# Hybrid decoder trunk: last stage's sums in PSUM on TensorE, and expert routing in two batches of four tiles

## The reference, cut to what matters

```python
x = x + mem_cross_attention(h, memn, w_mq, w_mkv, w_mo)
h = rmsnorm(x, norm_ffn)
# hier_moe: top-1 of 4 groups, then top-2 of the 8 experts in it
grp_prob = softmax(h @ w_rg + b_rg); p_grp, g_sel = top_k(grp_prob, 1)
sel = (h @ w_re + b_re) of the selected group
w_top, i_top = top_k(softmax(sel), 2); w_top /= sum(w_top)
gates = p_grp * w_top;  idx = g_sel * 8 + i_top
out = sum over the two chosen experts e of gates_e * (silu(h @ wg_e) * (h @ wu_e)) @ w_dn_e
x = x + out
return rmsnorm(x) * norm_final
```

## Time and profile before

| | |
|---|---|
| median of 3 runs | 1349.31 us |
| the profiled execution | 1345.35 us |
| its span | 1343.5 us |
| TensorE busy | 1187.0 us, 88% of the span |
| VectorE busy | 505.0 us, 38% |
| ScalarE busy | 395.5 us, 29% |
| GpSimd busy | 130.8 us, 10% |
| mean granted TensorE clock | 0.949 |

### The profile page before, as it was taken

One profiled execution on the slowest core, in us unless ns is written; L12 is line 12 of the kernel. 1 busy time (PEld: TensorE's weight loads), 2 busy tenths in 40 slices (PEclk: granted clock), 3 DMA queues, 4 the chain that ended last, 5 costly groups with the idle time before them and its releaser, 6 DMA issues.

```text
span 1343.5 us, 17627 instructions
## 1 busy us (share of the span) xinstructions
PE 1187.0 (88%) x7200; PEld 659.5 (49%) x7200; DVE 505.0 (38%) x1224; ACT 395.5 (29%) x753; POOL 130.8 (10%) x126
## 2 busy tenths in 40 slices
PE   5899999999999999997899998677759999999940
PEld 4444744447545898874554444345533333333310
DVE  5322314111798256754512221256632221222118
ACT  3102631113684231136641000474201111111115
POOL 1000011110000000011000000211011111111024
PEclk9799999999999999998999999799769999999975
DMA  5311112221125433303040003410149999999536
GB/s 178 110 32 33 32 53 75 75 75 53 32 71 242 114 80 123 119 2 126 1 157 1 0 0 131 188 48 32 48 173 417 412 417 416 423 418 412 218 151 257
DMA packets 67450, 199.55 MB, mean 149 GB/s; under 512 B 25780, under 2 KB 42404, under 8 KB 56612
## 3 DMA queue, kind: packets, MB, share of 16 engines
q1 hardware_dynamic: 59328, 181.39, 35.3%
q0 software_dynamic: 7456, 16.92, 3.3%
q10 hardware_dynamic: 580, 0.05, 0.0%
HBM read 172.63 MB, written 35.14 MB: 155 GB/s over the span
## 4 chain that ended last, share of the span: by engine, by line
PE 82%; DVE 9%; ACT 3%; issue 3%; DMA 2%; ACTq 0%; POOL 0%; DVEq 0%; POOLq 0%
PE bank L2285 28%; PE bank L1414 12%; PE bank L1475 7%; PE bank L1440 6%; PE bank L750 2%; PE bank L736 2%; PE bank L1490 2%; PE bank L1530 2%; PE bank L1400 2%; PE bank L2393 2%; PE bank L811 1%; PE bank L783 1%; PE bank L2274 1%; PE bank L841 1%; DVE arena L1661 1%
## 5 line engine op out<-in xcount | busy, mean ns | idle before, releaser
L2285 PE MATMUL bank<-arena 128*128 128x512 f32 (+3 forms) x1088 | 379.4, 509 | 1.6 <-DVE arena L2090 1.6
L2285 PEld LDWEIGHTS bank<-arena 128*128 128x128 f32 x1088 | 206.5, 191 | 169.3 <-issue 154.4
L1414 PE MATMUL bank<-arena 128*32 128x512 f32 x1536 | 171.0, 597 | 2.0 <-DVE arena L1193 2.0
L1414 PEld LDWEIGHTS bank<-arena 128*32 128x32 f32 x1536 | 50.7, 111 | 117.1 <-issue 117.1
L1866 ACT ACTIVATE arena<-bank 128x512 f32<-128x512 f32 (+1 forms) x64 | 32.9, 514 | 226.3 <-PE bank L2285 226.0
L1475 PE MATMUL bank<-arena 128*128 128x512 f32 x220 | 95.6, 592 | 0.0
L1440 PE MATMUL bank<-arena 128*32 128x512 f32 x768 | 87.4, 595 | 0.7 <-ACT arena L1102 0.7
L1202 DVE TENSOR_TENSOR arena<-arena,bank 128x256 f32<-128x256 f32 x25 | 10.5, 421 | 168.8 <-ACT arena L1098 155.7
L1475 PEld LDWEIGHTS bank<-arena 128*128 128x128 f32 x220 | 41.3, 190 | 49.7 <-issue 49.7
L1854 ACT ACTIVATE arena<-arena 128x1024 f32<-128x1024 f32 x26 | 27.4, 1054 | 127.2 <-DVE arena L1262 106.2
L1262 DVE TENSOR_TENSOR arena<-arena,bank 128x512 f32<-128x512 f32 x32 | 22.0, 688 | 112.5 <-PE bank L1475 87.8
(11 more groups left out here) (372 smaller groups left out, 1634.9 us busy)
## 6 DMA issues: line engine op xcount, KB each, us to landing
arena<-in_w_e_gu SPq DMA_DIRECT2D x27, 2048.0 KB, 15.8
arena<-in_w_e_dn SPq DMA_DIRECT2D x33, 1024.0 KB
arena<-in_w_in SPq DMA_DIRECT2D x11, 1024.0 KB, 5.4
arena<-y_d SPq DMA_DIRECT2D x8, 1024.0 KB, 5.0
arena<-hz_d SPq DMA_DIRECT2D x4, 1792.0 KB, 8.1
arena<-in_w_e_gu SPq DMA_DIRECT2D x6, 1024.0 KB
arena<-in_w_e_gu SPq DMA_DIRECT2D x12, 512.0 KB
pk_d<-arena SPq DMA_DIRECT2D x8, 640.0 KB, 2.9
```

Source lines behind the costliest of these rows:

```text
L1414: ins = mm(bank[part, :], hgT[:, k, part], w_gu(es[i] % NB, k), start=(k == 0), stop=(k == KT - 1))
L2285: ins = mm(psum[PROJ_BANKS[u % 3]][0:rows, 0:n], lhs(k), rhs(k), start=(k == 0), stop=(k == KT - 1))
```

## The change

Routing keeps its arithmetic and is cut in two batches of BT = 4 tiles. `route(m)` ends with the experts' maxima and indices. `choose(b)` makes the expert numbers and one-hot rows of four tiles at once; `ranks(b)` gets the ranks of four tiles by one product with the triangle and products of ones with the counts of each earlier tile, in banks 5 and 6; `place_tokens(b)` does the placing for four tiles in operations four times as wide; `table(b)` sums 8 products in bank 1, which holds the whole table at the end. `choose(0)` stands at the end of VectorE's step 8, `ranks(0)` at the end of TensorE's step 9, `place_tokens(0)` in step 11 behind the last normed rows and before `route(7)`. After the loop TensorE does the products for the earlier tiles of batch 1, `table(0)`, `ranks(1)`, the totals and `table(1)`. `probs_transposes(it)` moves ahead of `out_product(it-2, 1)`.

In the last stage VectorE makes `w_diag[m]`, diagonal matrices of the first gate. TensorE puts x2 into a bank by a product with the identity and adds the first expert's rows by a product with `w_diag[m]`. VectorE combines the second expert's rows with the bank, in two halves. ScalarE's `weigh` and GpSimd's add are gone.

```diff
             def route(m):
                 dve.wait_ge(s["t_rl"], m + 1)
-                link(v.tensor_tensor(lg[:, m], psum[7][:, 0:NR], br, ALU.add))
+                v.tensor_tensor(lg[:, m], psum[7][:, 0:NR], br, ALU.add).then_inc(s["t_slt"], 1)
+                dve.wait_ge(s["t_slt"], m + 1)
...
+            def choose(b):
+                ms = slice(BT * b, BT * b + BT)
+                link(v.tensor_copy(sixb, six[:, ms, 0:TK]))
+                link(v.scalar_tensor_tensor(eid_all[:, ms], bc(gself[:, ms], 2, [P, BT, TK]), float(EPG), sixb,
                                             ALU.mult, ALU.add))
+                link(v.tensor_tensor(oh, bc(io_f[:, 0:NE], 1, [P, BT * TK, NE]),
+                                     bc(flat(eid_all[:, ms]), 2, [P, BT * TK, NE]), ALU.is_equal))
+                v.tensor_tensor(asum[:, ms], oh[:, 0:BT * TK:TK], oh[:, 1:BT * TK:TK], ALU.add).then_inc(s["t_as"], 1)
+
+            def place_tokens(b):
+                ms = slice(BT * b, BT * b + BT)
+                n8 = [P, BT * TK, NS_]
+                rank, toks = flat(rank_all[:, ms]), flat(vt[:, ms])
+                dve.wait_ge(s["t_r_rk"], b + 1)
+                link(v.tensor_tensor(rtmp, oh.rearrange("p (m k) e -> p m k e", k=TK),
+                                     bc(rk(b).rearrange("p (m e) -> p m e", m=BT), 2, [P, BT, TK, NE]), ALU.mult))
+                link(v.tensor_reduce(rank, rtmp.rearrange("p m k e -> p (m k) e"), AX.X, ALU.add))
+                link(v.scalar_tensor_tensor(sb_i, flat(eid_all[:, ms]), float(CAP), rank, ALU.mult, ALU.add))
+                link(v.tensor_scalar(pub_i[:, 0], sb_i, P - 1, None, ALU.bitwise_and))
+                link(v.tensor_scalar(pub_i[:, 1], sb_i, 7, None, ALU.logical_shift_right))
+                link(v.tensor_copy(pub_f, pub_i))
+                link(v.tensor_tensor(ohb[b], bc(io_f, 1, [P, BT * TK, P]), bc(pub_f[:, 0], 2, [P, BT * TK, P]),
                                      ALU.is_equal))
+                link(v.scalar_tensor_tensor(v1b, rank, float(CAP), toks, ALU.is_lt, ALU.mult))
+                link(v.scalar_tensor_tensor(v2b, rank, float(CAP), toks, ALU.is_ge, ALU.mult))
+                link(v.scalar_tensor_tensor(v2b, rank, float(CAPX), v2b, ALU.is_lt, ALU.mult))
+                slots = rhb[b][:, :, 0:NS_]
+                link(v.tensor_tensor(slots, bc(io_f[:, 0:NS_], 1, n8), bc(pub_f[:, 1], 2, n8), ALU.is_equal))
+                link(v.tensor_tensor(slots, slots, bc(v1b, 2, n8), ALU.mult))
+                v.tensor_tensor(rhb[b][:, :, NS_:NTAB], oh, bc(v2b, 2, [P, BT * TK, NE]),
+                                ALU.mult).then_inc(s["t_pl"], 1)
...
                     normed_rows(it - 3)
+                if it == NT + 3:
+                    place_tokens(0)
                 if 0 <= it - 4 < NT:
                     route(it - 4)
...
-                if 0 <= it - 4 < NT:
-                    place_tokens(it - 4)
                 if it + 1 < NT:
                     inverse_sums(it + 1)
+                if it == BT + 4:
+                    choose(0)
+
+            choose(1)
+            place_tokens(1)
+            dve.wait_ge(s["t_r_rk"], 4)
+            link(v.tensor_copy(tab, psum[1][:, 0:NTAB]))
             rows_from(v, link, slice(0, NS_), tab[:, 0:NS_])
...
+            def before(b, m, start):
+                to = max(BT * b, m + 1) - BT * b
+                return mm(rk(b)[:, to * NE:].rearrange("p (m e) -> p m e", e=NE), ones[:, :],
+                          bc(asum[:, m], 1, [P, BT - to, NE]), start=start, stop=(m == BT * b + BT - 2))
+
+            def ranks(b):
+                pe.wait_ge(s["t_as"], b + 1)
+                own = asum[:, BT * b:BT * b + BT].rearrange("p m e -> p (m e)")
+                mm(rk(b), triu_s[:, :], own, start=(b == 0), stop=False)
+                for m in range(BT * b, BT * b + BT - 1):
+                    ins = before(b, m, False)
                 ins.then_inc(s["t_r_rk"], 1)
...
+                if it < NT:
+                    probs_transposes(it)
                 if 0 <= it - 2 < NT:
                     out_product(it - 2, 1)
-                if 0 <= it - 4 < NT:
-                    ranks(it - 4)
-                if it < NT:
-                    probs_transposes(it)
                 if 0 <= it - 3 < NT:
                     rows_transposes(it - 3, 1)
                     router(it - 3)
+                if it == BT + 5:
+                    ranks(0)
+
+            def table(b):
+                pe.wait_ge(s["t_pl"], b + 1)
+                for i in range(BT * TK):
+                    ins = mm(psum[1][:, 0:NTAB], ohb[b][:, i], rhb[b][:, i], start=(b + i == 0),
+                             stop=(b == 1 and i == BT * TK - 1))
+                return ins
+
+            for m in range(BT):
+                before(1, m, m == 0)
+            table(0)
+            ranks(1)
+            pe.wait_ge(s["t_slt"], NT)
+            for m in range(NT):
+                ins = mm(psum[7][:, 0:NE], ones[:, :], asum[:, m], start=(m == 0), stop=(m == NT - 1))
+            ins.then_inc(s["t_r_rk"], 1)
+            table(1).then_inc(s["t_r_rk"], 1)
...
         def dve_tail3(dve, v, link, inverse_rms):
+            for m in range(NT):
+                ins = v.tensor_scalar(w_diag[:, m], ident[:, :], wts[:, 0, m:m + 1], None, ALU.mult)
+                ins.then_inc(s["t_r_dve"], 1) if m == NT - 1 else link(ins)
...
+                    y_wait(dve, m)
+                    for hf in range(2):
+                        dve.wait_ge(s["f_p"], 2 * m + hf + 1)
+                        cols = slice(hf * HALF, (hf + 1) * HALF)
+                        v.scalar_tensor_tensor(x2[:, m, cols], yg[m][:, 1, cols], wts[:, 1, m:m + 1],
+                                               psum[2 * (m % 4) + hf][:, :], ALU.mult, ALU.add).then_inc(s["f_c"], 1)
...
+        def pe_tail3(pe, mm):
+            def start(m):
+                for hf in range(2):
+                    if m >= 4:
+                        pe.wait_ge(s["f_c"], 2 * (m - 4) + hf + 1)
+                    mm(psum[2 * (m % 4) + hf][:, :], ident[:, :], x2[:, m, hf * HALF:(hf + 1) * HALF],
+                       start=True, stop=False)
+
+            pe.wait_ge(moe["y"], 2 * UN)
+            for m in range(4):
+                start(m)
+            pe.wait_ge(s["t_r_dve"], 6)
+            for m in range(NT):
+                if m >= 4:
+                    start(m)
+                y_wait(pe, m)
+                for hf in range(2):
+                    mm(psum[2 * (m % 4) + hf][:, :], w_diag[:, m], yg[m][:, 0, hf * HALF:(hf + 1) * HALF],
+                       start=False, stop=True).then_inc(s["f_p"], 1)
```

More of the change, by code:

```diff
@@ L903, in hybrid_trunk @@
         gex = rt(NT, NG)
-        sixf = rt(TK)
         io_i = rt(P).bitcast(i32)
         vt_i = rt(NT, TK).bitcast(i32)
-        oh, rtmp = rt(TK, NE), rt(TK, NE)
+        BT = 4
+        oh, rtmp = rt(BT * TK, NE), rt(BT, TK, NE)
         gsum = rt(NG, EPG)
-        asum, apre = rt(NT, NE), rt(NT, NE)
+        asum = rt(NT, NE)
+        sixb, v1b, v2b = rt(BT, TK), rt(BT * TK), rt(BT * TK)
+        sb_i, pub_i, pub_f = rt(BT * TK).bitcast(i32), rt(2, BT * TK).bitcast(i32), rt(2, BT * TK)
+        ohb = [view(o_tmp + (5 + i) * D, BT * TK, P) for i in range(2)]
+        rhb = [view(o, BT * TK, NTAB) for o in (o_g1 + 4 * T, o_tmp + 7168)]
+        assert 4 * T + BT * TK * NTAB <= 4 * T + 2 * GW and BT * TK * NTAB <= 568
+        rk = lambda b: psum[5 + b][:, 0:BT * NE]
         kp = region(o_cx + 1024, o_tmp)
@@ L1309, in route @@
                 link(v.max_index(six[:, m], smx[:, m], sel[:, m]))
-                link(v.tensor_copy(sixf, six[:, m, 0:TK]))
-                link(v.scalar_tensor_tensor(eid_all[:, m], gself[:, m:m + 1].to_broadcast([P, TK]), float(EPG), sixf,
-                                            ALU.mult, ALU.add))
-                link(v.tensor_tensor(oh, bc(io_f[:, 0:NE], 1, [P, TK, NE]), bc(eid_all[:, m], 2, [P, TK, NE]),
-                                     ALU.is_equal))
-                v.tensor_tensor(asum[:, m], oh[:, 0], oh[:, 1], ALU.add).then_inc(s["t_as"], 1)
@@ L1317, in place_tokens @@
-            def place_tokens(m):
-                dve.wait_ge(s["t_r_rk"], m + 1)
-                if m >= 1:
-                    link(add_table(v))
-                link(v.tensor_tensor(rtmp, oh, bc(psum[7][:, 64:64 + NE], 1, [P, TK, NE]), ALU.mult))
-                v.tensor_reduce(rank_all[:, m], rtmp, AX.X, ALU.add).then_inc(s["t_slt"], 1)
-                dve.wait_ge(s["t_slt"], m + 1)
-                link(slot_steps(v, link, m))
-                link(v.scalar_tensor_tensor(val2, rank_all[:, m], float(CAP), vt[:, m], ALU.is_ge, ALU.mult))
-                link(v.scalar_tensor_tensor(val2, rank_all[:, m], float(CAPX), val2, ALU.is_lt, ALU.mult))
-                v.tensor_tensor(rhs_t[:, :, NS_:NTAB], oh, bc(val2, 2, [P, TK, NE]), ALU.mult).then_inc(s["t_pl"], 1)
-                if m + 1 < NT:
```

(35 more changed lines are left out.)

17 lines of the change are left out of this document (5 added, 12 removed).

## The result

The changed kernel takes 1326.51 us (median of 4 runs, 1324.72 to 1329.52) against 1348.61 us (1345.33 to 1351.01) for the kernel before on the same chip: a ratio of 0.9841, with an interval of 0.9818 to 0.9864. The forecast was 1325.5 us, with a range of 1315 to 1338. The profiled execution took 1329.52 us, its span 1327.7.

What follows compares the result with a forecast made beforehand. Routing was taken as bound by a ring of waits, no engine full, the last stage by its per-tile chain across engines. Routing's 14.0 us and the last stage's 9.8 off the span gave 1321.5, at the median 1325.5 us (range 1315 to 1338).

Steps and rivals of the forecast that it cites:

- ahead of the first router: Routing loop, before the first router product: the moved transposes of probabilities give 0.4 us.
- two full steps: Routing loop: two windows of 14.0 us between router products become 11.5, saving 2.5 us each.
- step from 925.30: Routing-loop step without scores, clock 0.88 before: 11.2 us at full clock, saving 2.8; at the old clock 1.6 less.
- step of 10.19: Routing-loop step that took 10.19 us before: loses only 0.8 us.
- step of 12.52: Routing-loop step where TensorE waited for VectorE: 8.1 us without place_tokens, saving 4.4 (3.0 if the clock falls).
- step of 9.73: Routing-loop step where TensorE waited for route before its rank product: 5.7 us, saving 4.0; at half clock 2.5 less.
- end of routing: Last router start to table, after the loop: 19.6 us against 14.1, 5.5 lost; at full clock about 0.5.
- the ring: Routing loop: chain of waits through TensorE and VectorE that sets a full step, 14.0 us, to become 11.5.
- (c): Routing's four full steps: half clock from the first router on, steps about 18 us instead of 14, total 1375; chance 0.03.
- (a): Routing's full steps: another member keeps the ring at about 13 us; routing gives 8, total 1331.5; chance 0.24.
- (b): Last stage: TensorE becomes the bound at half clock, 13 us lost, time 1348; chance 0.05.
- (d): Routing batches: placing four tiles in series loses more than the loop saves; at 8 us more, 1333.5; chance 0.08.

Runs made afterwards that it cites:

- first pair: First profiles of the kernel before and the changed kernel, nothing else altered: executions of 1345.35 and 1329.52 us.
- second pair: Both kernels, before and changed, profiled again unchanged: executions of 1348.2 and 1328.4 us.
- transposes_back: Changed kernel with the transposes of probabilities put back behind the second output product: 1332.46 us, ratio 0.9882 to the kernel before.
- fill_all: Changed kernel with idle TensorE products both in waits of the routing loop and behind the loop: 1317.44 us, ratio 0.9774 to the kernel before.
- fill_end: Changed kernel with idle TensorE products only behind the routing loop: 1322.33 us, ratio 0.9811 to the kernel before.

## Why the prediction was right

**Both parts, and their sum.** The forecast was 14.0 us of routing and 9.8 of the last stage. Measured were 9.0 and 9.35 in the first pair of profiles, 13.3 and 9.8 in the second, and 22.1 for the whole in the medians against 23.8. In the spans of the profiles 23.8 us were forecast, 15.8 came in the first pair and 19.8 in the second. That the time came out within 1 us (1325.5 against 1326.51) is thus partly luck. Against the profile that they were made from, the routing terms below fell short by 5.0 us, the last stage by 0.4, and the experts' 1.3 us were not in the sum at all. In the other direction, that profile was itself too good for its kernel by some 4 us in the same stretch: of 29 further runs of the kernel before, eight took 1344.4 to 1345.6 us, as it did, and 21 took 1347.3 to 1350.9. The forecast took its saving from that short profile and its level, 3.96 us higher, from the median, so the falls that the profile lacked and those that the forecast left out of after nearly cancel.

Two of the forecast's own signs came out narrowly or not at all. The last router product came 12.7 us earlier in its stretch (17.0 in the second pair), not 19. The first gather came 7.8 us earlier in the span of the first pair, where less than 8 was named as a sign of being wrong; counted from tile 0's output product it was 9.0, and 11.6 and 13.3 in the second pair.

**Routing, term by term** (us saved, from the starts of the router products in each pair of profiles; the sums are of unrounded terms):

| term | forecast | first pair | second pair |
|---|---|---|---|
| ahead of the first router | 0.4 | -2.4 | 0.4 |
| first step | 2.1 | 2.0 | 2.3 |
| two full steps | 5.0 | 5.0 | 5.4 |
| step from 925.30 | 2.8 | 0.4 | 0.5 |
| step of 10.19 | 0.8 | -0.8 | -0.8 |
| step of 12.52 | 4.4 | 4.2 | 4.6 |
| step of 9.73 | 4.0 | 4.3 | 4.8 |
| end of routing | -5.5 | -3.7 | -3.7 |
| sum | 14.0 | 9.0 | 13.3 |

In the first pair every term whose clock was full is right within 0.3 us, and so is what stood behind them: the ring loses four small VectorE operations, table and ranks, and 0.9 us by the moved transposes (shown by transposes_back). The three that fell short are clock terms. Ahead of the first router, the output product of tile 1 took 3.78 us and the values before it 2.03: 2.7 us that the first profile of before did not pay, and its second did, so in the second pair this term is right. For the step from 925.30 I took full clock, though the row of before had 0.88; "at the old clock 1.6 less" was the better value, and with 0.75 it came out at 2.4 less. That product was slow in both profiles of before as well (3.17 and 3.68 us). The step behind it was 11.03 us at 0.85. fill_all shows the sizes at full clock: 10.82 and 9.42 us, where 11.2 and 9.4 were forecast. What failed of the forecast is thus one step: the choice of full clock for the step from 925.30 and the one behind it. The forecast's condition of rival (c), a clock below 0.8 over all full steps, did not come: three of them had 1.00.

**The end of routing.** The prices held: place_tokens 4.8 us as forecast (959.21 to 964.0, and 969.44 to 974.24), its 1024-wide one-hot 1.23 us for 1.26, a table product 3.66 us for 4.4 at a clock of 0.54, ranks(1) 1.9 for 2.2. From router to gather it was 19.24 us, where the 19.6 to the table alone, plus the 1.5 to the gather, would have made 21.1. What is lost there against before is mostly the half clock: fill_end takes the stretch to 17.03 and fill_all to 16.66, so TensorE's clock is worth 2.2 to 2.6 of the 3.7. At full clock fill_all lost 1.1 us against before; the forecast said about 0.5 there, where its own prices add up to 1.0. And the low clock reached further than I had followed it: the first expert product, which I had left at its length ("its TensorE chain is unbroken"), took 10.00 us instead of 8.64, and 7.09 with the clock kept.

**The last stage.** Forecast were 1330.7 - 1297.2 = 33.5 us from the first load to the end; 33.9 were measured, with 3.43 us a tile from tile 4 (3.44) and scales at 1284 ns. The start of the identity products was the open term (1293.3 to 1297.2, 1295.5 taken). TensorE took the early end: it began 0.6 us after the end of VectorE's last copy, having idled 1.35 us, and had the full clock. That brought nothing more, because the loads decide what comes next: tile 1 landed 9.4 us after the first load, and tile 4's identity product began at 16.2, where the forecast had 9.1 and 15.8. Of the rule about a fetch behind a taken branch (the Trainium skill, Runtime: NRT & Kernel Launch, Instruction fetch mechanics) the trace fits one half: VectorE, on the same path, idled 3.92 us on "issue" ahead of its diagonals, and the queues that carry instructions moved four packets from 1287 to 1289, though the trace does not say for which engine. TensorE showed no such stall. The diagonals were done at 1293.3, before the first tile, as forecast, so this cost nothing either.

**The rivals.** (a) A ring of about 13 us: no, 11.5, and transposes_back shows 12.4 without the move. (b) Half clock in the last stage: no, 0.94 and 0.99. (c) Half clock from the first router on: no; its mechanism does act, in single steps. (Its terms add up to 1378 us, not 1375.) (d) Batches dearer than priced: no, they came out 1.8 us cheaper.

**What stays open.** Why the clock fell where it did. Falls are seen behind waits of 3.48, 1.64 and of only 0.36 us, while full steps with waits of 0.5 to 0.7 us keep 1.00 in after and have a short fall in other profiles (fill_all at 884.98, the second profile of before at 888.63); and the same code had and had not a fall in the same place in two executions. The runs show that work in the waits makes falls fewer, not what decides between one wait and another.

## What to carry to other kernels

Read the granted clock of every window before pricing its steps, and price a step that had less than 1.00 at that clock or lower; here a change that shortened other engines' work left TensorE's falls where they were or moved them, and their cost reached into the next stage. Where TensorE waits again and again for a few tenths to a few microseconds in a chain that sets the end, try idle products in many of those waits, not in one: here that won 9 us more, where the whole change had won 22. And profile the kernel before twice: its first profile here was 4.3 us off its second in the stretch that the sum was made from.

## What the runs showed of the hardware

- Idle TensorE products made the kernel faster: 1326.5 to 1317.4 us with 40 more matmuls, the granted clock in the end of routing going from 0.54 to 1.00 and the first expert product from 10.00 to 7.09 us.
- Removing one fall of the clock brought nothing in the median (1326.73 us); others appeared later in the same profile (output product at 943.85, 3.62 us; last router product, 3.63 us).
- The same routing code had a fall in one execution and none in another: 120.76 us at a mean granted clock of 0.87, and 125.03 us at 0.81.
- GpSimd adds of 128x1024 float32 beside VectorE: a VectorE operation of the same width with both tensors in SBUF went from 1.28 to 1.88 us in the mean and 3.07 at most, one of 512 with a tensor in PSUM stayed at 0.74, and the adds themselves took 2.86 us.
- Behind the skipped overflow branch VectorE lost 3.9 us on "issue" where TensorE, on the same path, idled 1.35 us, part of it in waiting for VectorE's copy.
